# Moving four of eight blocks of a gate from the mixing stage into the recurrent stage, in a hybrid decoder block

## What is computed

```
h    = RMSNorm(x) * (1 + scale1) + shift1
proj = h @ W_in        # attention q, k, v; DeltaNet q, k, v; z; beta; alpha; gate_a (1024); gate_b (1024)
y_a  = sliding_window_attention(...) @ W_A
od   = gated_delta_rule(...)                     # 8 heads of 128, a recurrence over chunks of 64 tokens
od   = RMSNorm_per_head(od) * silu(z)
y_b  = od @ W_B
mix  = (sigmoid(gate_a) * y_a + sigmoid(gate_b) * y_b) @ W_out
x    = x + gate1 * mix
h2   = RMSNorm(x) * (1 + scale2) + shift2
x    = x + gate2 * PEER(h2)                      # 8 heads, top-16 of 128 x 128 experts
```

## Time and profile before

| | |
|---|---|
| median of three runs | 2327.51 us |
| the profiled execution | 2327.64 us, span 2325.8 us |
| TensorE busy | 2234.4 us, 96% |
| VectorE, ScalarE, GpSimd busy | 1700.6 (73%), 913.4 (39%), 711.6 us (31%) |
| mean granted clock of TensorE | 0.985 |
| recurrent stage | 387.5 to 702.8 us |
| mixing up to the output projection | 702.8 to 848 us |
| output projection, second norm, queries | 848 to 992 us |
| experts | 992 us to the end |

### The profile page before, as it was taken

How to read it: one execution, slowest core, us unless ns; L and a number is a source line. 1 busy time by engine, 2 the same in 40 slices (tenths; PEclk the granted TensorE clock), 3 DMA queues, 4 the chain that set the end, 5 groups by cost and what they waited for, 6 DMA issues and landing times.

```text
span 2325.8 us, 35740 instructions
## 1 busy us (share of the span) xinstructions
PE 2234.4 (96%) x14109; PEld 1942.4 (84%) x14109; DVE 1700.6 (73%) x3216; ACT 913.4 (39%) x1592; POOL 711.6 (31%) x646
## 2 busy tenths in 40 slices
PE   6899998999989999989999999999999999999998
PEld 2687777888877789889999999888888888888887
DVE  4388775554456745179999998788887888887887
ACT  2234666123214425255555554333333333333332
POOL 0356683000000000036675334433333333333320
PEclk9999998999999999999999999999999999999999
DMA  8333431101113232244444668989998899999893
GB/s 291 92 110 105 130 119 46 29 20 46 38 47 127 91 127 73 73 144 130 134 142 144 199 208 290 357 323 318 321 320 309 317 324 321 316 343 325 316 323 122
DMA packets 224998, 442.35 MB, mean 190 GB/s; under 512 B 22424, under 2 KB 138305, under 8 KB 224577
## 3 DMA queue, kind: packets, MB, share of 16 engines
q1 hardware_dynamic: 177040, 270.19, 35.2%
q0 software_dynamic: 45568, 163.60, 19.8%
q10 hardware_dynamic: 2224, 6.29, 0.7%
HBM read 394.16 MB, written 45.88 MB: 189 GB/s over the span
## 4 chain that ended last, share of the span: by engine, by line
PE 37%; DVE 19%; issue 0%; DMA 0%; ACT 0%; POOL 0%; DVEq 0%; ACTq 0%; POOLq 0%
PE bank L2078 23%; DVE hot_j L2294 6%; PE bank L2064 4%; PE bank L2062 4%; PE bank L2063 4%; DVE hot_i L2289 3%; PE bank L1946 2%; DVE eq L2262 1%; DVE eq L2258 1%; DVE pick L2264 1%; DVE ti L2231 1%; DVE ti L2224 1%; DVE sc_work L2225 1%; DVE pos L2231 1%; DVE pos L2224 1%; DVE tv L2228 1%
## 5 line engine op out<-in xcount | busy, mean ns | idle before, releaser
L1908 POOL TENSOR_TENSOR ua_lo<-ua,ua_hi 128x512 fp32r<-128x512 f32 x128 | 191.7, 1518 | 394.4 <-ACT ua L2113 394.1
L2078 PE MATMUL bank<-vt_hi,wg_hi 128*128 128x512 f32 x768 | 248.0, 404 | 5.7 <-DVE wg_lo L2348 5.4
L1901 POOL DMA_INDIRECT ug<-in_peer_u_dram,gidx x128 | 145.4, 1136 | 329.6 <-DVE ug L2304 326.2
L2078 PE MATMUL bank<-vt_lo,wg_hi 128*128 128x512 f32 x768 | 239.0, 392 | 0.0
L2078 PE MATMUL bank<-vt_hi,wg_lo 128*128 128x512 f32 x768 | 238.0, 391 | 0.0
L2330 DVE TENSOR_TENSOR vt_lo<-vt_raw,vt_hi 128x1024 fp32r<-128x1024 f32 x128 | 156.4, 1222 | 92.0 <-ACT vt_hi L2200 92.0
L1930 POOL DMA_INDIRECT vg<-in_peer_v_dram,gidx x128 | 131.2, 1025 | 238.0 <-DVE g_acc L2319 226.0
L1976 PE MATMUL bank<-h_hi,ua_hi 128*128 128x384 f32 x512 | 179.8, 351 | 0.7 <-ACT ha L2126 0.6
L2062 PE MATMUL bank<-h_hi,uT_hi 128*128 128x384 f32 x512 | 176.8, 345 | 0.0
L2211 ACT ACTIVATE wg_hi<-wt 128x384 fp32r<-128x384 f32 x128 | 67.4, 526 | 277.0 <-DVE wt L2343 277.0
L2200 ACT ACTIVATE vt_hi<-vt_raw 128x1024 fp32r<-128x1024 f32 x128 | 135.2, 1057 | 98.3 <-PE bank L2078 98.3
(11 more groups left out here) (444 smaller groups left out, 5542.5 us busy)
## 6 DMA issues: line engine op xcount, KB each, us to landing
u_raw<-in_peer_u_dram SPq DMA_DIRECT2D x128, 512.0 KB, 6.5
vt_raw<-in_peer_v_dram SPq DMA_DIRECT2D x128, 512.0 KB, 6.0
gates<-g_stage SPq DMA_DIRECT2D x12, 2048.0 KB, 8.8
gate<-gates SPq DMA_DIRECT2D x32, 768.0 KB, 8.0
pj_raw<-in_w_in_dram SPq DMA_DIRECT2D x16, 1024.0 KB, 5.3
ada_w<-in_w_ada_dram POOLq DMA_DIRECT2D x32, 512.0 KB, 4.6
hid_keep<-ha POOLq DMA_DIRECT2D x64, 192.0 KB, 4.3
hl<-hid_keep SPq DMA_DIRECT2D x64, 192.0 KB, 8.2
```

What stands on the lines that cost most here:

```text
L1901: nc.gpsimd.indirect_dma_start(ug[s % RING][:], None, u_rows, bass.IndirectOffsetOnAxis(m.gidx[:, s:s + 1].bitcast(U32), 0)).then_inc(s_ug ...
L1908: nc.gpsimd.tensor_tensor(ua_lo[b % 2][:, 4 * q:4 * q + 4, :], ua[b % 2][:, 4 * q:4 * q + 4, :], ua_hi[b % 2][:, 4 * q:4 * q + 4, :].bitca ...
L2078: ins = pe.matmul(y_bank[t][q][:], w[n % 2][:, tok], v[n % 2][:, 512 * q:512 * q + 512], start=(first and i == 0), stop=(last and i == 2))
```

## The change

Four of the eight blocks of gate_b (the last four, its slabs 2 and 3) are made by the fillings of the recurrent stage: FILLS goes from 15 to 19 (and the split block is number 19), a non-last tile has 120 products of filling, the last 96. Their sigmoids go to DRAM with those of gate_a, and SyncE loads them into `sig_b[2]` and `sig_b[3]` in the mixing. The fillings are dealt out anew over the places of a tile, one more split is made on each engine per tile, in VectorE's case inside the inverse's level 1. The mixing loses slabs 6 and 7; B goes from 8 to 6, OUT from 12 to 10. The norms are dealt out as 0; 1, 2; 3, 4; 5; 6, 7 after slabs 0 to 4. The splitting of `od` into y_hi and y_lo moves from iteration 6 (B - 2) to iteration 5 (B - 1). In both norms the scale by 1/n and eps are taken into ScalarE's root, which reads the sum from PSUM; the VectorE instruction between them goes.

```
+MOVED = 4
...
+m.eps = m.small("eps", [P, 1])
...
 w_in = a["w_in"].rearrange("o (k p) n -> p (o k) n", p=P)
-FILLS = 2 * DNH - 1
+FILLS = 2 * DNH - 1 + MOVED
...
     def load(f):
-        c = COL_Z + P * f if f < DNH else COL_GA + P * (f - DNH)
+        if f < DNH:
+            c = COL_Z + P * f
+        elif f < 2 * DNH - 1:
+            c = COL_GA + P * (f - DNH)
+        elif f < FILLS:
+            c = COL_GB + P * (f - 2 * DNH + 1 + KC - MOVED)
+        else:
+            c = COL_GA + P * (DNH - 1)
...
                 last.then_inc(z["KK"], 1)
-        fill(0 if last_tile else 4)
+        fill(4)
...
                 last.then_inc(z["QK"], 1)
-        fill(8)
+        fill(12)
...
                 last.then_inc(z["P"], 1)
-            if l < 4:
-                fill(12 if l == 0 else 0 if last_tile else 3)
+            if l < 5:
+                fill((8 if last_tile else 14) if l == 0 else 4 if last_tile else 6)
...
             last.then_inc(z["uw"], 1)
-        fill(8 if last_tile else 10)
+        fill(8 if last_tile else 13)
...
             if c == 0:
-                fill(0 if last_tile else 9)
+                fill(4 if last_tile else 9)
...
         tok = slice(P * t, P * t + P)
-        b0 = 4 * t
+        b0 = 5 * t
...
         high(b0 + 3)
+        gate(b0 + 2)
+        high(b0 + 4)
         act.wait_ge(z["uw"], t * 2 + 2)
         for q in range(2):
             hs = slice(G * q, G * q + G)
             nc.scalar.activation(u[:, hs, :], bank[2 + q][:].rearrange("p (h n) -> p h n", h=G), ACT.Copy)
             last = nc.scalar.activation(wT[:, hs, :], bank[q][:].rearrange("p (h n) -> p h n", h=G), ACT.Copy)
         last.then_inc(z["uwe"], 1)
-        gate(b0 + 2)
+        gate(b0 + 3)
         if t < NT - 1:
-            high(b0 + 4)
+            high(b0 + 5)
...
                 ins.then_inc(z["D"], 1)
-        low(b0 + 3)
+            if l == 1:
+                low(b0 + 3)
+        low(b0 + 4)
...
             if cc == 0 and t < NT - 1:
-                low(b0 + 4)
+                low(b0 + 5)
...
 gates = part(w_in, COL_GB)
-slabs = gates[:1] + part(w_a, 0) + gates[1:] + part(w_b, 0)
+slabs = gates[:1] + part(w_a, 0) + gates[1:2] + part(w_b, 0)
...
 m.s_sk = m.sem("mix_sk")
-GATES, A, B, OUT, WQ, N = (0, 5, 6, 7), 1, 8, 12, 16, 24
-z = {n: m.sem("mix_" + n) for n in "sig rest rest_sig ahi alo ohi olo xt mixed mhi mlo x2 x2a sq ms msr sqrt ht h hh split2 os om oe or on".split()}
+GATES, A, B, OUT, WQ, N = (0, 5), 1, 6, 10, 14, 22
+z = {n: m.sem("mix_" + n) for n in "sig sigb eps rest rest_sig ahi alo ohi olo xt mixed mhi mlo x2 x2a sq ms sqrt ht h hh split2 os om or on".split()}
 bank = m.bank
 def heads(s):
-return ((0,), (1,), (2, 3), (4,), (5,), (6, 7))[s] if s < 6 else ()
+return ((0,), (1, 2), (3, 4), (5,), (6, 7))[s] if s < 5 else ()
...
             sp.dma_start(m.x2T[:].rearrange("p k n -> p (k n)"), m.xT_dram).then_inc(z["xt"], 16)
+        if s == B + 1:
+            for i in (2, 3):
+                sp.wait_ge(z["mixed"], 2 * i)
+                sp.dma_start(sig_b[i][:], m.sig_dram[2 * i + 3:2 * i + 5, :, :].rearrange("k p n -> p k n"))\
+                    .then_inc(z["sigb"], 16)
...
         if n >= 2:
-            pe.wait_ge(z["oe"], n - 1)
+            pe.wait_ge(z["or"], n - 1)
...
         if i:
-            act.wait_ge(z["mixed"], 2 * i)
+            act.wait_ge(z["mixed"], 2 * (s - 1))
...
     def root(n):
-        act.wait_ge(z["oe"], n + 1)
-        nc.scalar.activation(o_rs[:, n % 2, :], o_rs[:, n % 2, :], ACT.Sqrt).then_inc(z["or"], 1)
+        act.wait_ge(z["om"], n + 1)
+        if n == 0:
+            act.wait_ge(z["eps"], 1)
+        if n >= 2:
+            act.wait_ge(z["on"], n - 1)
+        nc.scalar.activation(o_rs[:, n % 2, :], bank[4 + n % 2][:], ACT.Sqrt, scale=1.0 / DNK,
+                             bias=m.eps[:]).then_inc(z["or"], 1)
...
                 square(n + 2)
-        if s == 6:
+        if s == B - 1:
...
-        act.wait_ge(z["msr"], i + 1)
-        nc.scalar.activation(rs[:, TOKENS[i]], rs[:, TOKENS[i]], ACT.Sqrt).then_inc(z["sqrt"], 1)
+        act.wait_ge(z["ms"], KC + EARLY * i)
+        nc.scalar.activation(rs[:, TOKENS[i]], bank[6 + i][:, TOKENS[i]], ACT.Sqrt, scale=1.0 / D,
+                             bias=m.eps[:]).then_inc(z["sqrt"], 1)
...
-    def mean(n):
-        dve.wait_ge(z["om"], n + 1)
-        if n >= 2:
-            dve.wait_ge(z["on"], n - 1)
-        v.tensor_scalar(o_rs[:, n % 2, :], bank[4 + n % 2][:], 1.0 / DNK, EPS, ALU.mult, ALU.add).then_inc(z["oe"], 1)
-
...
         i = s - A if s < B else s - B
+        if s >= B + 2:
+            dve.wait_ge(z["sigb"], 16 * (i - 1))
...
                 v.tensor_tensor(mix[:, k, :], mix[:, k, :], sig_b[i][:, half, :], ALU.add).then_inc(z["mixed"], 1)
+    v.memset(m.eps[:], EPS).then_inc(z["eps"], 1)
...
         for n in heads(s):
-            mean(n)
             normed(n)
-        if s == 6:
+        if s == B - 1:
...
-        dve.wait_ge(z["ms"], KC + EARLY * i)
-        v.tensor_scalar(rs[:, TOKENS[i]], bank[6 + i][:, TOKENS[i]], 1.0 / D, EPS, ALU.mult, ALU.add).then_inc(z["msr"], 1)
```

More of the change, by code:

```diff
@@ L2371, in kernel_program @@
         m.clear()
-        m.sig_dram = nc.dram_tensor("sig_keep", [DNH, P, SEQ], F32, kind="Internal").ap()
+        m.sig_dram = nc.dram_tensor("sig_keep", [DNH - 1 + MOVED, P, SEQ], F32, kind="Internal").ap()
         slabs = mix_slabs(a)
```

## The result

| | before | changed |
|---|---|---|
| median of 20 runs each, taken in turns | 2331.03 us | 2335.78 us |
| lowest and highest | 2324.50, 2336.86 | 2330.06, 2340.26 |
| profiled execution (span) | 2327.64 (2325.8) | 2331.84 (2330.0) |

The ratio is 1.002, 95% interval 1.0012 to 1.0029: the change costs 0.2%, 4.7 us, and the profiled pair shows the same, 4.2 us. The forecast was 2335.4 us, +7.9 us or +0.34%. That the time agrees to 0.4 us is luck: the kernel before came out 3.5 us higher in these runs than in the first three, and the difference is 3.2 us smaller than forecast. By the bound of 0.3% the change can't be told from none, a case to which I gave 0.36 against 0.60 for slower.

What follows compares the result with a forecast made beforehand. TensorE, busy 96% of the span, was taken as the bound, its work order setting both stages' ends. -21.8 + 18.9 + 9.0 + 1.8 = +7.9 us on 2327.5 gave 2335.4 us; 8 in 10 range 2331 to 2340.5.

Steps and rivals of the forecast that it cites:

- Part 1: Mixing: 96 products (two slabs of 48) leave TensorE's path, -21.8 us.
- part 3: Mixing, before the second branch: TensorE stalls for the eight y_lo, +9.0 us.
- part 4: Mixing, behind the stall: the granted clock falls and slows products, +1.8 us, with 0 and 2.6 as ends.
- the norms' slack: Mixing, VectorE: the head norms end 1.3 us early, so they cost nothing; lateness beyond that lengthens the stall.
- The case that I held against the rule: Trace start: from 15.21, after 8.09 us of waiting, products ran at clock 1.00; without a fall the sum is 1.8 lower.
- Part 2: Recurrent stage: the same 96 products as filling cost +18.9 us, with 17.5 and 20.5 as ends.
- I take 0: Recurrent stage: where its own slow clock stretches fall can shift by 1.6 us either way, counted as 0.
- stays covered: Before the second branch: only the old wait of 0.6 us stays, -2.9 us, 2324.6 us; chance 5%.
- filling nearly free: Recurrent stage: idle time takes most fillings, so the move costs 7 to 8 us there; 2317 to 2324 us; chance 5%.
- more than one thing late: Head norms miss their 1.3 us, or fillings wait for split or bank in each tile; 2340 us; chance 12%.
- Within the noise, with a slow stretch fewer: Whole kernel: forecast mechanism, but no clock fall and one slow stretch fewer; 2331 to 2334.4 us; chance 30%.

Runs made afterwards that it cites:

- stall_filled: Changed kernel plus 40 products nobody reads, placed before the wait on y_lo; mixing 132.3 us against 134.1, median 2336.29 us.
- fill_only: The change's recurrent stage put into the kernel before, whose mixing still multiplies all eight gate_b blocks; median 2343.82 us.
- y_early: Changed kernel with the y_hi and y_lo splits one iteration earlier on ScalarE and VectorE; median 2333.43 us.
- before_again: Kernel before, no edit, traced a second time; median 2330.63 us, recurrent stage 315.4 us.

## Why the prediction was right, and where not

- **Part 1, -21.8, and part 3, +9.0: right, number and mechanism.** With part 4 they make -11.0, and the mixing went from 145.1 to 134.1. The wait is 9.6 us (forecast 9 to 10); the norms' slack was 1.23 (1.3); with the mean back it is overrun, as said. Four edits of that chain moved the wait to 15.3, 6.1, 2.2 and 5.5.
- **Part 4, +1.8: right**, 1.8 by stall_filled. The Trainium skill (TensorE: Matmul & The Clock Gate, section "HAM oscillation — how this bites in real kernels") says that a gap throttles the work behind it; this trace agrees, 799.7 to 809.9 at 0.50, of which only 3.76 us were work. The case that I held against the rule was misread: I took the granted clock of 1.00 behind the wait of 8.09 us, from 15.21, for full speed. Sixteen like products stand there, and their weight loads are 0.85 us apart up to 21.1 and 0.43 us from then on (below). Further on the same products are 0.85 apart in a window with a granted clock of 0.50, from 48.4, and 0.43 apart behind it. So the work behind that wait ran at half speed for some 6 us, though the view says 1.00. Whether the clock was low before the wait already isn't shown; but nothing in this trace spoke for a stall without slow work behind it.
- **Part 2, +18.9: the work right, the clock's term mis-sized; this is the step that failed.** The stage grew by 15.3. I had written that I would be wrong if it grew by less than 16, and for this stage I was. The levels (5.13 for 5.1) and the waits came as counted. The mis-sized term is the one on the stage's own slow stretches, "I take 0", with 1.6 either way: slow time fell from 27.3 to 20.5 us, and that gave 3.4 us back. The tiles show it (table below). Between tiles of the old and the new order with as much slow time (the new tile 1 from fill_only, the new tile 3 from y_early, whose recurrent stages are that of the changed kernel) the growth is 4.6, 4.6, 4.5 and 5.0, 18.7 in all (I had 4.6 three times and 5.1). Where the same code of a tile had one slow stretch of 6.8 instead of 3.4 us it took 1.6 to 1.7 longer. In the changed kernel tiles 1 and 3 had the shorter one, and had the longer one in the kernel before. The last tile of before_again is the exception among the tiles: its start had none, and its 3.4 us lay at the second chunk, from 695.3.
- **The sum.** +7.9 less 3.4 for the clock and 0.2 for the products is 4.3, the 15.3 less 11.0 between the cuts; the profiled pair has +4.2.

Weight loads of these products in the kernel before: behind the wait, then around 48.4, with the window there (us, busy of PE, granted clock, DMA share, GB/s):

```profile
18.58 0.13 PEld L229 LDWEIGHTS bank<-wada,silu_c 128*1 128x1 f32 x1 [0.72 <-issue]
19.43 0.13 PEld L229 LDWEIGHTS bank<-wada,silu_c 128*1 128x1 f32 x1 [0.73 <-issue]
...
22.42 0.08 PEld L229 LDWEIGHTS bank<-wada,silu_c 128*1 128x1 f32 x1 [0.34 <-issue]
22.85 0.08 PEld L229 LDWEIGHTS bank<-wada,silu_c 128*1 128x1 f32 x1 [0.34 <-issue]
...
49.49 0.13 PEld L229 LDWEIGHTS bank<-wada,silu_c 128*1 128x1 f32 x1 [0.73 <-issue]
50.34 0.13 PEld L229 LDWEIGHTS bank<-wada,silu_c 128*1 128x1 f32 x1 [0.73 <-issue]
52.38 0.08 PEld L229 LDWEIGHTS bank<-wada,silu_c 128*1 128x1 f32 x1 [0.34 <-issue]
52.81 0.08 PEld L229 LDWEIGHTS bank<-wada,silu_c 128*1 128x1 f32 x1 [0.34 <-issue]
...
48.40:51.80 3.40, 3.12 (x4) 0.50 0.57 159
```

The four tiles of the recurrent stage, each from its first one-column product to that of the next (the last to the second cut), in us, with the slow time in it:

| kernel | tile 0 | tile 1 | tile 2 | tile 3 |
|---|---|---|---|---|
| before | 79.5 (7.1) | 79.3 (6.8) | 77.7 (3.4) | 73.4 (6.8) |
| before_again | 82.1 (12.5) | 77.7 (3.4) | 79.3 (6.8) | 72.7 (3.4) |
| changed | 84.1 (7.2) | 82.3 (3.4) | 82.2 (3.4) | 76.7 (3.4) |
| fill_only | 82.8 (4.3) | 83.9 (6.8) | 82.2 (3.4) | 76.7 (3.4) |
| y_early | 86.6 (12.5) | 82.3 (3.4) | 82.3 (3.4) | 78.4 (6.8) |

Where the slow stretches lie is seen in their windows, of the kernel before and of the changed one, columns as in the earlier trace rows:

```profile
475.10:481.90 6.80, 6.80 (x34) 6.80 (x34) 1.68 (x12) 2.01 (x5) 0.00 (x0) 0.50 0.00 0
557.00:560.40 3.40, 3.40 (x19) 3.40 (x18) 2.21 (x12) 2.52 (x8) 0.00 (x0) 0.50 0.00 0
632.10:638.90 6.80, 6.80 (x34) 6.80 (x34) 1.64 (x12) 1.97 (x4) 0.00 (x0) 0.50 0.01 4
```

```profile
482.30:485.70 3.40, 3.40 (x18) 3.40 (x17) 1.97 (x12) 2.53 (x7) 0.00 (x0) 0.50 0.00 0
564.20:567.60 3.40, 3.40 (x19) 3.40 (x18) 1.70 (x11) 2.24 (x6) 0.00 (x0) 0.50 0.00 0
646.10:649.50 3.40, 3.40 (x18) 3.40 (x17) 1.42 (x11) 1.76 (x4) 0.00 (x0) 0.51 0.00 0
```

The first one-column products of two tiles of the kernel before and of one of the changed:

```profile
472.38 4.34 PE L1070 MATMUL bank<-ones,dn_sq 128*128 128x1 f32 x32
551.72 3.63 PE L1070 MATMUL bank<-ones,dn_sq 128*128 128x1 f32 x32
...
477.28 3.63 PE L1079 MATMUL bank<-ones,dn_sq 128*128 128x1 f32 x32
```

Each stretch is near the start of a tile, with TensorE busy throughout. They are not "in the runs of one-column products", as I had written: the one from 475.1 began in such a run, those from 557.0 and 482.3 behind it, over transposes. Before, there were 17.0 us of them in tiles 1 to 3, after it 10.2.

Did the denser filling shorten them, or the place at which they caught the tile? All 13 traces together have 39 starts of the tiles 1 to 3. Where a stretch began 2.7 to 3.7 us after the tile's first one-column product it lasted 6.8 us (8 times), where it began 4.1 to 5.5 us after, 3.4 us (30 times), and once there was none; both lengths occur in the old order of the stage and in the new one. So the length goes with the place and not with the filling. The new order lay well in these traces: its three starts, 82.3 us and 82.2 us apart, had the short stretch each in seven of nine traces with the change's recurrent stage (20.5 us of slow time), while fill_only and y_early had one long one each (21.5 and 29.7); the three with the old order had 27.3, 27.3 and 29.7. Nothing in the prediction said where its tiles would be caught, so the 3.4 us are luck of the place. What sets that place is open: this is read off the traces, and no experiment moved a tile on purpose without changing its work.

The rivals: "stays covered" fell by the wait of 9.6, "filling nearly free" by fill_only, "more than one thing late" by the slack of 1.23 and the absence of waits on fillings. "Within the noise, with a slow stretch fewer" is what came in size, 4.2 to 4.7 us, though the clock did fall behind the stall and the slow time was shorter by two stretches' worth. It had deserved more than its 30%: the slow time in that stage was a row of the trace, its half lost was 14 us, and the forecast lay only 1 us above the bound.

## What to carry to other kernels

When work is moved away from between a producer and its consumer, ask what it covered: here two slabs of products hid a chain of sigmoid, copy, low part and eight splits, and 9.0 of 21.8 us gained went into it; moving the splits ahead of work that isn't due, and waiting piece by piece, gave it back. An edit measured alone (0.9 us for the roots) can be worth seven times as much beside the change that puts it on the path. And before calling a term zero, look at how much of the stage runs at the low clock: here each of three tile starts could have 3.4 us of it more or less, 1.6 to 1.7 us of time each, and my bounds allowed for one.

## What the hardware showed that I had not expected

- The granted clock was 0.50 in stretches in which TensorE was busy for all of 3.40 or 6.80 us, during or just behind one-column products: to be busy was not enough.
- How long such a stretch lasted, 3.4 or 6.8 us, went with where it caught the start of the tile (4.1 to 5.5, or 2.7 to 3.7 us behind its first one-column product), with the same work there.
- A granted clock of 1.00 at the very start of a trace can be wrong: up to 21.1 us like products were 0.85 us apart, as they were later at 0.50, then 0.43. The distance between like products is the check.
- Slow time makes much of the difference between executions of one kernel: of the 20 of the changed one, the seven of 2330.1 to 2332.3 us had a mean granted clock of 0.985 or 0.986, the thirteen of 2335.4 to 2340.3 us 0.982 or 0.983. In the traces 30.7 us of slow time lie ahead of a first cut at 388.4 to 390.3, and 38.6 to 43.5 us ahead of one at 392.3 to 394.1, by the same code.
- A wait of 9.6 us gave a slow stretch of 10.2, most of it over before TensorE had work again: the clock's part of the stall was 1.8 us, a sixth of it.
